# Fourteen down-projection phases of a two-layer transformer as seven half-sized block products

## The reference, cut to what matters

```
mlp (2 of them):  x = ALPHA * x + relu(h @ w1)^2 @ w2      w1: 1024 x 4096, w2: 4096 x 1024
ffn (4 of them):  x = x + 0.5 * (silu(h @ wg) * (h @ wu)) @ wd      wd: 2816 x 1024
```

## Time and profile before

| | |
|---|---|
| median of 3 runs | 3758.97 us (3756.57 to 3764.41) |
| the profiled execution, span from first to last instruction | 3762.2 us |
| PE busy | 3680.7 us, 98% of the span |
| DVE busy / ACT busy / POOL busy | 1884.2 us (50%) / 1433.2 us (38%) / 152.6 us (4%) |
| mean granted TensorE clock | 0.995 |

### The profile page before, as it was taken

The page is one execution under the profiler, slowest core; times in us unless marked ns, Lnnn a source line. Parts: engine busy times, 40 slices in busy tenths (PEclk is TensorE's granted clock), DMA queues, the critical chain, the costliest instruction groups (busy, mean ns, idle before and its releaser), DMA issues.

```text
span 3762.2 us, 46018 instructions
## 1 busy us (share of the span) xinstructions
PE 3680.7 (98%) x18208; PEld 3004.4 (80%) x18208; DVE 1884.2 (50%) x2668; ACT 1433.2 (38%) x2168; POOL 152.6 (4%) x149
## 2 busy tenths in 40 slices
PE   9999899999999999999999999999999999999999
PEld 7776788887678888888877898888888877888887
DVE  4455644366754445433367564334433476564333
ACT  3345332336534223332255443323332354443322
POOL 0001000000100000000000310000000000310000
PEclk9999999999999999999999999999999999999999
DMA  4000222222013223222221012222322221012221
GB/s 180 34 34 34 79 91 100 93 98 93 21 53 116 90 101 110 92 101 95 90 92 48 12 63 101 90 101 84 112 91 100 73 103 48 18 57 101 101 91 72
DMA packets 45285, 306.91 MB, mean 82 GB/s; under 512 B 5136, under 2 KB 5520, under 8 KB 10640
## 3 DMA queue, kind: packets, MB, share of 16 engines
q1 hardware_dynamic: 45072, 303.97, 22.9%
HBM read 301.86 MB, written 2.10 MB: 81 GB/s over the span
## 4 chain that ended last, share of the span: by engine, by line
PE 85%; DVE 9%; ACT 4%; issue 1%; DMA 0%; DVEq 0%; POOL 0%; ACTq 0%; SPq 0%; POOLq 0%
PE ps L445 83%; ACT arena L1159 2%; PE ps L454 2%; DVE split L2092 2%; DVE arena L2096 2%; DVE arena L2092 2%; DVE X L2096 1%; ACT split L1159 1%; DVE arena L2943 1%; ACT L1159 0%; DVE arena L2088 0%; DVE small L2108 0%; DVE arena L2120 0%; DVE arena L2100 0%; DMA X<-in_x 0%
## 5 line engine op out<-in xcount | busy, mean ns | idle before, releaser
L445 PE MATMUL ps<-split 128*128 128x512 f32 (+2 forms) x13596 | 3086.5, 386 | 23.5 <-DVE X L2096 7.0
L445 PEld LDWEIGHTS ps<-split 128*128 128x128 f32 x13596 | 2479.1, 189 | 551.1 <-issue 48.8
L2092 DVE TENSOR_TENSOR split<-ring,split 128x1024 fp32r<-128x1024 f32 x554 | 676.1, 1220 | 1185.7 <-ACT split L1159 1168.2
L1159 ACT ACTIVATE split<-ring 128x1024 fp32r<-128x1024 f32 x554 | 582.8, 1052 | 1247.2 <-PE ps L445 1207.0
L445 PE MATMUL ps<-arena 128*128 128x128 f32 (+9 forms) x3344 | 487.1, 298 | 24.9 <-DVE arena L2092 9.7
L445 PEld LDWEIGHTS ps<-arena 128*128 128x128 f32 (+2 forms) x3344 | 395.6, 191 | 100.1 <-issue 68.7
L1159 ACT ACTIVATE arena<-ps 128x512 f32<-128x512 f32 (+6 forms) x580 | 298.0, 514 | 383.3 <-PE ps L445 217.9
L2092 DVE TENSOR_TENSOR arena<-arena 128x512 f32<-128x512 f32 (+5 forms) x254 | 150.6, 593 | 69.5 <-ACT split L1159 49.8
L1159 ACT ACTIVATE split<-arena 128x512 fp32r<-128x512 f32 x156 | 98.7, 633 | 165.3 <-DVE arena L2092 163.1
L2092 DVE TENSOR_TENSOR arena<-arena,ps 128x512 f32<-128x512 f32 x176 | 121.0, 688 | 41.3 <-PE ps L445 21.5
L2092 DVE TENSOR_TENSOR split<-arena,split 128x512 fp32r<-128x512 f32 x156 | 108.0, 692 | 64.2 <-ACT split L1159 61.6
(11 more groups left out here) (99 smaller groups left out, 968.7 us busy)
## 6 DMA issues: line engine op xcount, KB each, us to landing
ring<-in_wts SPq DMA_DIRECT2D x268, 1024.0 KB, 4.8
ring<-in_wts SPq DMA_DIRECT2D x25, 512.0 KB, 3.4
X<-in_x SPq DMA_DIRECT2D x4, 512.0 KB, 6.0
out<-arena SPq DMA_DIRECT2D x4, 512.0 KB, 2.6
ring<-in_wts SPq DMA_DIRECT2D x2, 784.0 KB, 5.6
C<-in_cb SPq DMA_DIRECT2D x1, 1403.5 KB, 14.5
ring<-in_wts SPq DMA_DIRECT2D x2, 576.0 KB, 10.5
C<-in_cb SPq DMA_DIRECT2D x1, 512.0 KB, 6.4
```

Of the source, the lines that this page charges most:

```text
L445: return e.matmul(out, l, r, start=start, stop=stop, skip_group_check=True)
L1159: o.sig(a.activation(out, i, f, **kw), sig)
L2092: o.sig(v.tensor_tensor(out, a, b, op), sig)
```

## The change

Phases 0, 1 and 2 of each mlp and phases 0 and 1 of each ffn (6 + 8 = 14 phases) become a "unit". The hidden block A (512 tokens x 1024) and the weight block B (1024 x 1024) are cut in quarters, a11 to a22 and b11 to b22, and seven products of a quarter or a sum of quarters (`PRODUCTS`) take the place of eight. Each product is two pieces of 12 matmuls with 128 x 512. The last phase of each part stays two ordinary lins.

- The four weight quarters are four loads of 1 MB, which fill the ring. Four weight sums are made by DMAs that GpSimd issues with `accum_op=ALU.add`: t1 = b11 + b12 and t4 = b21 + the sum t2, both in a buffer `M.t14` that is first filled by another load from HBM ("again"); t3 = b12 + b22 and t2 = b11 + t3, both in place in the ring. Each DMA waits on GpSimd's queue for the one before it.
- Four input sums for f5, f6, f3 and f7 are made by GpSimd's `tensor_tensor` (semaphore "shape"), three of them in one buffer `M.sum`, so that the second and third wait until the form before them was split ("form").
- The hidden tiles are kept unsplit in `M.raw`; a quarter or sum is split ("formed") into one of four buffers by ACT ("fhi") and DVE ("form"). The first four forms of a unit are made in the steps of the last lins of `up(p + 1)` (`beside`), one in each step of the second lin in an mlp, one in every second step from the second lin on in an ffn (`spaced`); the other three in the unit. After the change a step q of `lin` ends with `next(beside)`.
- PSUM tiles of four products are read twice: once partly summed ("part"), once at the end. DVE adds them to X, or to a tile `P1` whose sum is put on X in six operations after the last unit.

```diff
+PRODUCTS = (("P1", "b11", "a11"), ("N5", "t1", "f5"), ("P6", "t2", "f6"), ("N3", "b22", "f3"),
+            ("P7", "t3", "f7"), ("P2", "b21", "a12"), ("N4", "t4", "a22"))
...
+    def unit(name, key, p, last, h, kbase, up):
+        nonlocal n, sums
+        U = lins[name] = Unit(name, h, p, p == last - 1)
+        for q, k0, c0 in (("b11", 0, 512), ("b12", 0, 0), ("b22", h, 0), ("b21", h, 512)):
+            U.loads[q] = load(f"{name}/{q}", key, kbase + k0, h, c0, 512)
...
+        for x, (_, b, f) in enumerate(PRODUCTS):
+            U.forms.append(form(f, (last - p) % 2, h, up))
+            for q in (0, 2):
...
+        for b in ("t1", "t2", "t3", "t4"):
+            for q in (0, 2):
+                U.pieces[at[b, q] - U.pieces[0].i].sum = (b, sums)
+        for q, b, added in (("b11", "t2", "t4"), ("b12", "t3", "t2"), ("b22", "b22", "t3"), ("b21", "b21", None)):
+            U.loads[q].end, U.loads[q].added = ("lo", at[b, 2] + 1), added and (added, sums)
...
+            if p < 3:
+                unit(f"dn{l}{p}", f"w2_{l}", p, 3, 4, 8 * p, f"up{l}{p}1")
+                continue
+            quarters = [form(a, 0, 4, f"up{l}{p}1") for a in ("a11", "a21", "a12", "a22")]
...
+        for r, (what, _, _) in enumerate(PRODUCTS):
+            f, begun = U.forms[r], {"N3": "N5", "P7": "P6", "P2": "P1", "N4": "P7"}.get(what)
+            x = tuple(K.m.formed(f))
+            e.wait_ge(S["form"], f.i + 1)
+            for p in U.pieces[2 * r:2 * r + 2]:
+                e.wait_ge(S["lo"], p.i + 1)
...
+                    if p.q == 0 and begun:
+                        e.wait_ge(S["part"], read[begun, t])
+                        of = K.turn[name, begun, t]
+                        K.turn[name, what, t] = Bank(of.t, of.i, of.n)
...
+                    for k in range(p.c):
+                        kk = p.k + k
+                        i = mm3(b.t[:, :], [v[:, kk, 128 * t:128 * t + 128] for v in x], [v[:, k, :] for v in w],
+                                kk == 0 and not begun, kk == U.h - 1)
...
+        if p.sum:
+            v = K.m.weights(p)
+            a.wait_ge(S[p.sum[0]], p.sum[1])
...
+    def form(f):
+        if f.after:
+            a.wait_ge(S["used"], f.after)
+        a.wait_ge(*emptied(f.up, 3))
+        if f.sum:
+            a.wait_ge(S["shape"], f.sum)
+        act(next(K.m.formed(f)), K.m.source(f), ACT.Copy, "fhi")
...
+    def unit(name, then=()):
+        ps, fs, then = lins[name].pieces, lins[name].forms, formed(then)
+        prime(name)
+        for r in range(7):
+            for p in ps[2 * r + 2:2 * r + 4]:
+                next(side, None)
+                next(side, None)
+                split(p)
+            if 1 <= r <= 3:
+                form(fs[r + 3])
+            elif r >= 4:
+                next(then, None)
+        flush()
...
-                t, b = K.m.tmp[:, m % 2, :], turn[f"up{l}{p}{c}", m]
+                b = turn[f"up{l}{p}{c}", m]
                 a.wait_ge(*b.full)
...
-                act(t, b.t[:, :], ACT.Relu, b)
-                act(K.m.U[p % 2][0][:, c * 4 + m, :], t, ACT.Square, "to_dve")
-                ucount += 1
+                act(K.m.tmp[:, m % 2, :], b.t[:, :], ACT.Relu, "relu")
...
-        for p in range(4):
-            if p < 3:
-                up(p + 1)
-            for c in range(2):
-                lin(f"dn{l}{p}{c}", embedded() if p + c == 3 and p == 3 else idle())
+        for p in range(3):
+            up(p + 1, formed(lins[f"dn{l}{p}"].forms[0:4]))
+            more = unit(f"dn{l}{p}", lins[f"dn{l}30"].forms if p == 2 else ())
...
+        def spaced(gen):
+            for _ in gen:
+                yield
+                yield
...
+        for p in range(2):
+            up(p + 1, spaced(formed(lins[f"fd{w}{l}{p}"].forms[0:4])))
...
+        for what, _, _ in PRODUCTS:
+            for t in range(2):
+                b = turn[name, what, t]
+                v.wait_ge(*b.full)
+                if what == "P1":
+                    if U.p:
+                        tt(y[:, t, :], y[:, t, :], b.t[:, :], ALU.add, "part")
+                    else:
+                        vcp(y[:, t, :], b.t[:, :], "part")
+                elif what == "N5":
+                    onto(2 + t, 0, b, 1, "part")
+                elif what == "P6":
+                    onto(t, 0, b, -1, "part")
...
+                next(beside, None)
...
-                t, k = M.tmp[:, m % 2, :], c * 4 + m
-                acted()
-                tt(t, t, t, ALU.mult)
-                tt(M.U[p % 2][1][:, k, :], t, f32(M.U[p % 2][0][:, k, :]), ALU.subtract, "u")
+                b = turn[f"up{l}{p}{c}", m]
+                told("relu")
+                stt(M.raw[(3 - p) % 2][:, c * 4 + m, :], b.t[:, :], 0.0, M.tmp[:, m % 2, :], ALU.max, ALU.mult, b)
...
+    def unit(name):
...
+        last = K.turn[U.forms[0].up, 3]
+        g.wait_ge(S[f"free{last.i}"], last.n + 1)
+        for x, (f, a, b, op) in enumerate(((1, "a21", "a22", ALU.subtract), (2, "sum", "a11", ALU.subtract),
+                                           (3, "sum", "a12", ALU.add), (4, "a11", "a21", ALU.subtract))):
+            f = U.forms[f]
+            if x == 0 and earlier:
+                g.wait_ge(S["form"], earlier.i + 1)
+            if x in (1, 2):
+                g.wait_ge(S["form"], f.i)
+            g.tensor_tensor(M.source(f), M.quarter(f, a), M.quarter(f, b), op).then_inc(S["shape"], 1)
+        n = U.h * 512
...
+        if before:
+            g.wait_ge(S["lo"], before.split["t4"])
+        g.dma_start(t14, W["wts"][U.loads["b11"].i]).then_inc(S["again"], 16)
+        here("b12")
+        g.wait_ge(S["again"], 2 * U.done - 16)
+        g.dma_start(t14, r["b12"], accum_op=ALU.add).then_inc(S["t1"], 16)
+        here("b22")
+        g.wait_ge(S["t1"], U.done)
+        g.dma_start(r["b12"], r["b22"], accum_op=ALU.add).then_inc(S["t3"], 16)
+        g.wait_ge(S["lo"], U.split["b11"])
+        g.wait_ge(S["t3"], U.done)
+        g.dma_start(r["b11"], r["b12"], accum_op=ALU.add).then_inc(S["t2"], 16)
+        g.wait_ge(S["lo"], U.split["t1"])
+        g.dma_start(t14, W["wts"][U.loads["b21"].i]).then_inc(S["again"], 16)
+        g.wait_ge(S["t2"], U.done)
+        g.wait_ge(S["again"], 2 * U.done)
+        g.dma_start(t14, r["b11"], accum_op=ALU.add).then_inc(S["t4"], 16)
...
+            if loads[ld.i - NS].added:
+                what, n = loads[ld.i - NS].added
+                s.wait_ge(S[what], n)
```

More of the change, by code:

```diff
@@ L107, in __init__ @@
         self.i, self.load, self.q, self.k, self.c = i, load, q, k, c
-        self.buf = self.after = None
+        self.buf = self.after = self.sum = self.form = None
 class Load:
@@ L211, in plan @@
 def plan():
-    lins, loads, turned, n = {}, [], [], 0
+    lins, loads, turned, forms, n = {}, [], [], [], 0
+    sums, shapes = 0, 0
     def load(name, key, k0, nk, c0, ncol):
@@ L266, in mlp @@
                     between=[(f"pt{l}", f"pT_{l}", 0, 2, 0, 512)] if p + c == 4 else ())
+            lins[f"dn{l}{p}0"].forms = quarters
+            for pc in lins[f"dn{l}{p}1"].pieces[-3:]:
+                pc.form = quarters[3].i + 1
+            for f in quarters:
+                f.end = n
         load(f"ln2{l}", f"ln2_{l}", 0, 1, 0, 2048)
@@ L295, in ffn @@
                 lin(f"fd{n_}{l}{p}{c}", f"fd{n_}_{l}", TILES[p], c * 512, 512, False, kbase=8 * p, between=[row] if p + c == 3 else ())
+            lins[f"fd{n_}{l}{p}0"].forms = quarters
+            for pc in lins[f"fd{n_}{l}{p}1"].pieces[-3:]:
+                pc.form = quarters[3].i + 1
+            for f in quarters:
+                f.end = n
     for l in range(2):
@@ L1176, in prime, with lin @@
             split(p)
-    def lin(name, evict=None, primed=False, mix=None, then=None, ms=range(4)):
+    def lin(name, evict=None, primed=False, mix=None, then=None, ms=range(4), beside=none):
         nonlocal side
@@ new lines, in unit @@
+    def unit(name, alpha, s, then=()):
+        nonlocal side
+        ps, fs, then, more = lins[name].pieces, lins[name].forms, formed(then), added(name, alpha, s)
+        prime(name)
+        for r in range(7):
+            for q in range(2):
+                if r == 0 or q == 0:
+                    next(side, None)
+                    next(side, None)
+                for p in ps[2 * r + 2 + q:2 * r + 3 + q]:
+                    split(p)
+            if r == 0:
+                flush()
+                side = more
+            if 1 <= r <= 3:
+                form(fs[r + 3])
+            elif r >= 4:
+                next(then, None)
+        return then
@@ L3221, in pool_program @@
         pass
+    for p in range(3):
+        unit(f"dn0{p}")
     O = K.o
@@ L3253, in pool_program @@
             rotation(3)
+    for p in range(3):
+        unit(f"dn1{p}")
     r0, r1 = K.SM[:, 24:28], K.SM[:, 20:24]
@@ L3260, in pool_program @@
     for l in range(2):
+        for p in range(2):
+            unit(f"fd1{l}{p}")
         g.wait_ge(*K.turn[f"hx{l}", 3, 1].full)
```

(2 more changed lines are left out.)

279 lines of the change are left out of this document (191 added, 88 removed).

## The result

The changed kernel takes **3845.3 us** (median of 4 runs, 3845.0 to 3847.7) against 3761.7 us before (4 runs beside it, 3756.6 to 3764.9): ratio **1.022**, 95% interval 1.021 to 1.024. The forecast was 3835 us, slower. The 336 matmuls went as planned (76 us), but new waits of TensorE and the slow work behind them cost about twice that (84 + 76 = 160 us).

A forecast was written before the change was run, and what follows sets the result against it. PE, busy for 98% of the span, was taken to bound the kernel. 3762 - 76 (matmuls) + 122 (waits) + 30 (clock) = 3838 us profiled, so 3835 us predicted; range 3715 to 3985 us for 8 in 10.

The forecast's parts named there:

- the waits: PE waiting for t1 and t2 in units: 16.4 us per mlp unit, 5.9 per ffn phase 1 unit, +122 us.
- the clock: PE at half clock behind a long wait: one loss of 3.0 us per late unit, 10 units, +30 us.
- The saving: 336 matmuls fewer on PE over 14 units, at 0.2265 us each: -76.1 us.
- The start of the chain: In an mlp, POOL issues its first DMA 2.7 us before the unit, behind its last sum; the load takes 4.8 us.
- T: Time in us counted from where PE ends the last up lin before a unit.
- X: Time of one accumulating DMA of 1 MB, issue to landing: 7.6 us taken, 4.0 to 10.4 as lower and upper end.
- I cost all of this at nothing: Added ACT and DVE work in units, DVE at most 5.5 us per product beside PE's 5.44, costs 0 us.
- The cheap add: Rival: accumulating DMAs of 1 MB take 4.0 to 5.8 us; 3717 us at 4.0, 3731 at 4.8; chance 0.19.
- The slow one: Rival: accumulating DMAs take over 10.4 us, limited by an adder or POOL's descriptor work; 3919 us at 10.4; chance 0.23.
- POOL and DVE hold each other up: Rival: POOL's three late sums each wait for a 1.2 us DVE operation; 37 us more, 3872 us; chance 0.04.

The follow-up runs named there:

- e1: Changed kernel with GpSimd issuing the load, t1 and t3 ahead of its late input sums in mlp units and ffn phase 1; 3693.4 us, ratio 0.982.
- e2: Changed kernel with the four accumulating DMAs made plain copies, so the weight sums are not computed; 3756.1 us, ratio 0.999.
- e5: Changed kernel with the load and adding DMAs issued ahead of the late input sums in the six mlp units only; 3730.8 us, ratio 0.993.
- e6: Changed kernel with the load and adding DMAs issued early in the four ffn units of phase 1 only; 3806.0 us, ratio 1.012.
- e8: Changed kernel with unread filler matmuls in PE's waits, and each following unit's first input sum held until the previous unit's last split; 3835.2 us, ratio 1.020.
- e7: Changed kernel with the first input sum of each following unit held until the last split of the unit before; 3843.7 us, ratio 1.022.

## Why the prediction was right

The sign, the mechanism and the size held. That the sum came out so near is in part luck: the waits were put some 19 us too low and the clock some 20 us too high.

**The saving: right.** -76.1 us forecast, -76.9 of PE's busy time in e1.

**The start of the chain: right; t1 is issued 0.8 us later than forecast.** With PE's end of the last up lin at 517.53 (529.82 - 6.85 - 5.44), the load is issued at T = -2.95 (forecast -2.7) behind sums of 2.4 us (2.5, from the earlier trace rows). The load then takes 5.86 us from its issue to t1's, 5.2 to landing, where 4.8 was taken from SP's loads; t1 is issued at T = 2.9 instead of 2.1.

**X: right for what it was used for.** From issue to the next issue t1 and t3 take 7.47 us each, t2 7.99 us from issue to ACT's split: 22.9 for the 3X that was put at 22.8, built as 2.0 + 2 x 2.8 each. So 7.6 was taken for the landing, and is right for landing and handoff together: the landing alone is 6.9 us for t1 and t4, the rest is the handoff on POOL. e2 shows the term behind it: without the add 4.5. The estimate of 6.8 us that the prediction drew from the Trainium skill (DMA: Bandwidth & Descriptors, Anatomy of one DMA — SWDGE (gpsimd) path, with both reads counted) agrees with the landing of 6.9; a chain pays the handoff of some 0.5 us on top.

**The waits: right in place, some 19 us short in sum.** P6 can start at T = 28.25 (forecast 27.3), so an mlp unit waits 17.4 us, 16.4 forecast (by e5, with 2.1 of clock taken off, 17.0). An ffn unit of phase 1 is idle 8.4, 6.9, 7.7 and 6.9 us, 5.9 forecast, for the load's extra time and, in the first of them, 9.0 us for the link t1 instead of 7.5; e6 has 9.8 in all. Less the clock it is 6 x 17.0 + 4 x 9.8 = 141 us, 122 forecast. Of the 19 us that are missing, some 9 lie behind the ffn waits, 2.3 us each. e8 accounts for 5.0 of them, in three of the four units, as PE waiting for DVE once the clock is held, where the forecast had DVE at nothing; the rest is open. Phase 0 of an ffn has no wait, as forecast.

PE's idle time grew by 122.0 us (203.5 less 81.5), the very number forecast for the waits. That is chance: N5 at low clock takes up 2.3 us of each mlp unit's wait, which the forecast had counted as idle, and the ffn waits make up for it.

**The clock: the step that was off.** "One loss of 3.0 us per late unit: 10 x 3.0 = +30 us" sized it from a stretch where nothing else was late. No run shows 3.0 us per unit. Measured are 8.5 to 12 us in all, 1.0 to 2.3 in an mlp unit and nothing in an ffn unit (e7, e8). PE's low clock behind the wait lies beside DVE's backlog: four splits and the PSUM reads that were held up follow each other without a gap. The step "I cost all of this at nothing", for DVE, at 5.5 us a product, holds where nothing is late (e1) and not behind a stall, where DVE has no slack to catch up from. PE's busy time hides this: it is 36.4 us higher than in e1, but part of that (7.70 for 5.44 us in N5, 2.3 us on average in six units) only fills time in which PE would have waited for t2, and part would have been a wait for DVE.

**The parts** then are 6 x 19.1 + 4 x 9.8 = 153.8 us by experiment against 6 x 19.4 + 4 x 8.9 = 152 forecast.

**The rivals.** The cheap add fell by X: it needed at most 5.8 us, and the links take 7.5. Its price was too low as well: at X = 4.8 the prediction had 3731, and e2, whose copies take 5.0 from issue to issue, takes 3756. By an estimate some 10 of these 25 us are the links (6 x 1.1 for the load, 6 x 3 x 0.2 for the copies); the rest no run takes apart. The slow one, X over 10.4, fell too. "POOL and DVE hold each other up" fell as written (the three late sums take 2.4 us each), but the reason given against it, POOL's even mean, says nothing of DVE: see below.

## What to carry to other kernels

Where sums and DMAs share one in-order queue, put first what has the longest chain behind it: three sums of 2.4 us ahead of four DMAs of 5 to 8 us made a loss of 84 us out of a gain of 68. Cost a chain of dependent DMAs from its issue, link by link (an adding one of 1 MB: 7.5 us; a copy: 5.0; the load: 5.9, each from issue to next issue), and see whether it ends before the first instruction that needs it. Behind a stall the low clock and the backlog of a feeding engine can overlap, as they did here: their costs did not add, and removing one of them showed nothing until the other had gone.

## What the runs showed of the hardware

**DVE waits for GpSimd.** The split that reads two inputs from SBUF took 3.58 us at 547.11, beside POOL's sum from 546.94 to 549.60; with that sum moved away it takes 1.22 us (e7, e8). It ended 1.1 us behind POOL's, about its own time, so it seems to have done its work after it. In the group of these splits this shows as a mean of 1274 ns against e8's 1222, easily overlooked:

```profile
L2246 DVE TENSOR_TENSOR split<-arena,split 128x1024 fp32r<-128x1024 f32 (+1 forms) x182 | 231.9, 1274 | 146.9 <-ACT split L1281 130.3
```

The Trainium skill (SBUF — State Buffer, Who interferes with whom) says that a DVE instruction with two SBUF inputs contends with a GpSimd one that reads SBUF. The trace agrees with the page. The prediction had taken it as DVE blocking GpSimd, and held that the trace did not bear it out, because POOL's operations had an even mean; but here POOL starts 0.17 us ahead and DVE pays, so the row to look at was DVE's.

**A copy within SBUF lands in 4.5 to 4.6 us** for 1 MB (e2), under a load's 4.8 from SP and 5.2 from GpSimd, and the add brings it to 6.9 to 7.9 us. t2, issued 0.55 us ahead of a reload, takes 7.99 us to ACT's split in the unit shown, where t1 and t3 take 7.47 to the next issue.
